# A hybrid backbone on one chip: input tiles, rope tables and scratch zeroing issued behind gates, and a planner that serves two transfer queues in turns

## The reference, cut to what matters

```python
for l in range(DEPTH):
    mod = silu_c @ w_mod[l] + b_mod[l]
    sh1, sc1, g1, sh2, sc2, g2 = split(mod, 6)
    hx = modulate(rms_norm(x, norm1_g[l]), sh1, sc1)
    if l % 2 == 0:                       # pooling || windowed attention
        out_x, out_c = even_mixer(hx, hc, mix_w_in[i], pool_w[i], ...)
    else:                                # pointwise, GLU, depthwise 31, LayerNorm, swish, pointwise
        out_x = conformer_conv(hx, *conv_args)
    x = x + g1 * out_x
    x = x + g2 * sq_relu_mlp(modulate(rms_norm(x, norm2_g[l]), sh2, sc2), mlp_w1[l], mlp_w2[l])
    # the context tokens take the same path in layers 0 and 1
return rms_norm(x, final_g)
```

## Time and profile before

| | |
|---|---|
| three runs | 3191.91, 3198.79, 3318.61 us (median 3198.79) |
| the profiled execution | 3186.52 us |
| its span, slowest core (core 4) | 3185.0 us; the others 3170.4 to 3184.0 us |
| PE busy in the span | 2963.4 us, 93% |
| DVE, ACT, POOL busy | 1890.2, 1206.6, 287.2 us |
| mean granted TensorE clock, core 4 | 0.990 |

### The profile page before, as it was taken

How to read it: one execution, slowest core, us unless ns; L and a number is a source line. 1 busy time by engine, 2 the same in 40 slices (tenths; PEclk the granted TensorE clock), 3 DMA queues, 4 the chain that set the end, 5 groups by cost and what they waited for, 6 DMA issues and landing times.

```text
span 3185.0 us, 42724 instructions; the slowest of 8 cores (3170.4 to 3185.0 us)
## 1 busy us (share of the span) xinstructions
PE 2963.4 (93%) x17933; PEld 1326.0 (42%) x18239; DVE 1890.2 (59%) x2941; ACT 1206.6 (38%) x1856; POOL 287.2 (9%) x545
## 2 busy tenths in 40 slices
PE   0699999999989999999999999999999999999997
PEld 0244344444444444444444443444443444344443
DVE  0455665665672457656567656665667346756567
ACT  1656821111264565211115658211116447411114
POOL 1102001111000000111100000011110010101000
PEclk9999999999999999999999999999999999999999
DMA  9327134444124662443422122244342472313102
GB/s 209 54 40 118 28 56 63 71 67 67 27 50 100 137 129 42 67 66 54 65 36 47 34 40 34 48 77 83 54 66 44 106 157 64 53 27 54 27 14 106
DMA packets 139968, 213.39 MB, mean 67 GB/s; under 512 B 18304, under 2 KB 66176, under 8 KB 139136
## 3 DMA queue, kind: packets, MB, share of 16 engines
q0 software_dynamic: 77904, 141.27, 28.1%
q1 hardware_dynamic: 61872, 69.38, 8.5%
HBM read 334.26 MB, written 17.56 MB: 110 GB/s over the span
## 4 chain that ended last, share of the span: by engine, by line
PE 83%; ACT 6%; DVE 6%; DMA 2%; SPq 2%; issue 1%; DVEq 0%; ACTq 0%
PE ps L157 83%; ACT ARENA L157 4%; DVE ARENA L157 4%; ACT H L157 2%; SPq L157 2%; DMA gscr<-ARENA 2%; DVE X L157 2%; DMA ARENA<-gscr 1%; DVE H L157 0%; ACT L157 0%; DVE MODV L157 0%; DVEq L1409 0%; DVE AB L157 0%; DVEq L155 0%; ACTq L155 0%
## 5 line engine op out<-in xcount | busy, mean ns | idle before, releaser
L157 PE MATMUL ps<-H,wr 128*128 128x512 bf16 (+1 forms) x7100 | 1528.0, 369 | 49.6 <-ACT ARENA L157 17.4
L157 ACT ACTIVATE ARENA<-ps 128x512 f32<-128x512 f32 (+5 forms) x939 | 586.6, 638 | 1557.9 <-PE ps L157 1537.0
L157 PEld LDWEIGHTS ps<-H,wr 128*128 128x128 bf16 x7280 | 697.1, 98 | 838.4 <-issue 34.0
L157 DVE SCALAR_TENSOR_TENSOR X<-ps,MODV,X 128x512 f32<-128x512 f32 (+1 forms) x1296 | 903.1, 718 | 203.5 <-PE ps L157 163.7
L157 PE MATMUL ps<-ARENA,wr 128*128 128x512 bf16 (+1 forms) x4511 | 1003.2, 368 | 6.7 <-DVE X L157 0.8
L157 DVE TENSOR_TENSOR ARENA<-ARENA 128x512 bf16<-128x512 f32 (+3 forms) x729 | 473.3, 661 | 577.8 <-ACT ARENA L157 577.4
L157 PEld LDWEIGHTS ps<-ARENA,wr 128*128 128x128 bf16 x4608 | 400.9, 98 | 591.5 <-DVE X L157 198.5
L157 POOL DMA_DIRECT2D wr<-w x256 | 135.7, 548 | 1326.4 <-PE ps L157 1257.5
L157 PE MATMUL ps<-ARENA 128*32 128x512 bf16 (+3 forms) x3038 | 228.8, 361 | 25.1 <-DMA ARENA<-gscr 12.8
L157 ACT ACTIVATE H<-ARENA,AB 128x512 bf16<-128x512 f32 (+1 forms) x296 | 191.2, 689 | 65.9 <-DVE ARENA L157 65.7
L157 DVE SCALAR_TENSOR_TENSOR ARENA<-X,AB,ARENA 128x512 f32<-128x512 f32 (+1 forms) x296 | 198.8, 710 | 23.4 <-ACT ARENA L157 13.8
(11 more groups left out here) (47 smaller groups left out, 715.3 us busy)
## 6 DMA issues: line engine op xcount, KB each, us to landing
wr<-w POOLq DMA_DIRECT2D x256, 256.0 KB, 6.6
wr<-w_mod POOLq DMA_DIRECT2D x192, 256.0 KB, 9.7
ARENA<-gscr SPq DMA_DIRECT2D x256, 135.0 KB, 3.6
wr<-pw POOLq DMA_DIRECT2D x48, 256.0 KB, 6.0
gscr<-ARENA SPq DMA_DIRECT2D x65, 128.0 KB, 1.9
X<-xp SPq DMA_DIRECT2D x4, 2048.0 KB, 35.2
outp<-ARENA SPq DMA_DIRECT2D x32, 256.0 KB, 2.2
ARENA<-ropet SPq DMA_DIRECT2D x8, 512.0 KB, 4.9
```

Source lines behind the costliest of these rows:

```text
L157: ins = getattr(e, it[1])(*it[2], **it[3])
```

## The change

The change has three parts.

**Gates at the start.** `load_x` and `DMA` take more keys to wait for. X0 is loaded only when the result of mod slab 1 (`modv`, 0, 1) is written; X1 only when the slab `w_u` has landed; X2 when `w_q` has landed; X3 when X1 has landed. The rope tables thereby come ahead of X0. `gpad`'s transfers also read the key (`X`, 3, 7), whose last writer by then is the mixer's output projection of tile 3; its memset is still free to go at any time.

**The planner.** Two queues (SP's, POOL's) are served in turns, piece by piece, by one server; a slab counts as four pieces, a load from the scratch as four pieces of double the bytes. A slot is counted free 0.13 us after its last user has been seen to end ("counts later bank reuse"), another 0.13 us are added before a PE operation that follows another engine, and some costs of issuing are changed.

**Pools.** The reserve of pool `f` falls from 3 to 1; the attention's `ub` pool gets a reserve of 3 and is strict (counts all older tiles); `rope_a` holds its two tiles together.

```diff
-LAT = {"pe": 0.20, "act": 0.125, "dve": 0.125, "pool": 0.15, "sp": 0.1}
+LAT = {"pe": 0.20, "act": 0.13, "dve": 0.13, "pool": 0.15, "sp": 0.1}
+LATPE = 0.13
...
+        def serve():
+            nonlocal seq
+            if dbusy[0]:
+                return
+            for k in (1 - dturn[0], dturn[0]):
+                if dqs[k]:
+                    o, last, dur = dqs[k].pop(0)
+                    dturn[0] = k
+                    dbusy[0] = True
+                    seq += 1
+                    heap_push(ev, (now + dur, seq, "free"))
+                    if last:
+                        seq += 1
+                        heap_push(ev, (now + dur + 2.0, seq, o))
+                    return
...
+                if type(o) is list:
+                    for vb in o[0].bufs:
+                        vb.left -= 1
+                        if vb.left == 0:
+                            for j in range(vb.size):
+                                vb.pool.free[vb.slot + j] = True
+                            vb.pool.settle()
+                    continue
...
-                    lat = 0.0 if (o.eng == "pe" and s_.eng == "pe") else (0.0 if o.dma is not None else LAT[o.eng])
+                    lat = LATPE if (o.eng != "pe" and s_.eng == "pe") else 0.0
...
-        f_p = gl.pool("f", NF, 512, 3)
+        f_p = gl.pool("f", NF, 512, 1)
...
-            ub_p = lay.pool("ub", 4, 256)
+            ub_p = lay.pool("ub", 4, 256, 3, True)
...
             if first:
-                load_x(1)
+                load_x(1, wu.keys())
                 norm(1, 0, 0)
+                load_x(2, wq.keys())
+                load_x(3, [("X", 1, 0)])
...
-                DMA("sp", lambda: "gr%d" % gr.slot, fl, rd + [("gpad",)], gr.keys(), 128 * 4 * w * 2, cost=1.9)
+                DMA("sp", lambda: "gr%d" % gr.slot, fl, rd + [("gpad",)], gr.keys(), 128 * 4 * w * 2 * 2, cost=1.8, pieces=4)
...
         load_x(4)
-        load_x(0)
-        for j in range(4):
-            mod_slab(0, j)
+        mod_slab(0, 0)
+        mod_slab(0, 1)
+        load_x(0, [("modv", 0, 1)])
+        mod_slab(0, 2)
+        mod_slab(0, 3)
...
-                                       for (a, b) in ((0, GL), (GL + S, GC), (GC + L, GW))], zb.keys(), [("gpad",)], 100000, cost=0.3)
+                                       for (a, b) in ((0, GL), (GL + S, GC), (GC + L, GW))], zb.keys() + [("X", 3, 7)], [("gpad",)], 3000000, cost=15.0)
```

More of the change, by code:

```diff
@@ L337, in __init__, with add @@
         self.phase_pools = []
-    def add(self, eng, emit, reads, writes, cost, dma=None, table=None, bias=0, soft=(), hold=()):
+    def add(self, eng, emit, reads, writes, cost, dma=None, table=None, bias=0, soft=(), hold=(), pieces=1):
         o = Op()
@@ L535, in schedule @@
                 done += 1
-                for vb in o.bufs:
-                    vb.left -= 1
-                    if vb.left == 0:
-                        for j in range(vb.size):
-                            vb.pool.free[vb.slot + j] = True
-                        vb.pool.settle()
+                seq += 1
+                heap_push(ev, (now + LATPE, seq, [o]))
                 for s_ in o.succ:
                     s_.npred -= 1
-                    lat = 0.0 if (o.eng == "pe" and s_.eng == "pe") else (0.0 if o.dma is not None else LAT[o.eng])
+                    lat = LATPE if (o.eng != "pe" and s_.eng == "pe") else 0.0
                     s_.ready = max(s_.ready, now + lat)
@@ L770, in PE, with DMA @@
             return R.add("pe", emit, reads, writes, cost, bias=bias, hold=hold, soft=R.after(dst))
-        def DMA(q, chan, f, reads, writes, nbytes, cost=None, soft=(), bias=0):
+        def DMA(q, chan, f, reads, writes, nbytes, cost=None, soft=(), bias=0, pieces=1):
             def emit(Sd):
@@ L775, in emit @@
                 Sd.dmas(q, Sd.chan(ch), f(), phys(reads), phys(writes))
-            return R.add(q, emit, reads, writes, cost if cost is not None else (1.0 if q == "pool" else 0.08), dma=nbytes, soft=soft, bias=bias)
+            return R.add(q, emit, reads, writes, cost if cost is not None else (0.55 if q == "pool" else 0.4), dma=nbytes, soft=soft, bias=bias, pieces=pieces)
         MMC = 0.2157
```

45 lines of the change are left out of this document (26 added, 19 removed).

## The result

The changed kernel takes 3098.38 us in the median of four runs (3097.57 to 3099.54), the kernel before 3188.41, 3191.91 and 3198.79; the ratio is 0.9704 (95% interval 0.9683 to 0.9724). In some executions of any of these kernels the cores of one die are granted a lower clock and take longer; such executions and cores are left out of every comparison here. I had forecast 3128, with 3104 to 3152 as the range: the gain is 95 us between the means, where my sum had 66, and more than half of it comes from where I had not looked.

The account below looks back on a forecast made before the run. PE was busy 2963 of 3185 us, so only 222 us of idle could be won. Terms -69 + 6 + 3 + 1 + 1 - 8 = -66 gave 3120.5; 7.5 added for runs above the profiled one made 3128, range 3104 to 3152.

Parts of the forecast that it names:

- The start: Start of layer 0: gated loads bring the first matmul with w_u from 131.3 to 62 us, a term of -69 us.
- M: The first matmul with w_u, at 131.25 us before; forecast at 62 us, bounded by 57 and 73.
- +3 ACT cover in mixer 0: Mixer of layer 0: norms of tiles 1 to 3 on ACT, now behind M, cost +3 us, bounds 0 and +17.
- +6 +3 +1: Costs put behind M: norm matmuls on PE +6.1 us, ACT's norms +3, gates behind M +1.
- The sign that I had named: Test of ACT's cover: wrong if PE's waits for ARENA tiles from ACT double between M and the MLP.
- The gates behind M, +1: Layer 0 after M: X1 there at 72 us, w_q at 74.3, both in time by 2 us; +1 us (0 to +8).
- The MLP of layer 0 idles 3.7 of 535 us, so nothing is to be had there: MLP of layer 0: PE's small idle time was taken to leave no gain there.
- The convolutions, -8: Planner's other orders, against 53.6 us of PE idle in the two convolutions: -8 us (-25 to +12).
- Zeroing, +1: Zeroing stores start when X3 is final, some 35 us of work before the slot's reuse: +1 us (0 to +10).
- The late start: Rival: slower weights' queue puts M at 70 and the mixer pays ACT's work in full; 3146 us, chance 0.18.
- The good planner: Rival: half of the convolutions' idle goes, -25 us instead of -8; 3111 us, chance 0.15.
- The slower case: Rival: fewer usable f slots double idle in the first mixer and both convolutions; 3200.5 us, chance 0.02.

Follow-up runs that it names:

- b_zt: The kernel before with only the zeroes moved to 64 columns of their own instead of a slot of f: 3152.43 us, ratio 0.9866.
- a_zt: The changed kernel, gates kept, with only the zeroes in columns of their own instead of a slot of f: 3098.40 us, ratio 0.9703.
- b_gates: The kernel before with only the gates of X0 to X3 and of the zeroing stores, old planner and pools: 3170.54 us, ratio 0.9934.
- b_zlate: The kernel before with only the zeroing (memset and three stores) moved behind the last write of X3: 3161.09 us, ratio 0.9890.
- a_f3: The changed kernel with the reserve of pool f back at 3 slots for older tiles instead of 1: 3137.77 us, ratio 0.9819.

## Why the prediction was wrong, point by point

- **The start** was right in size. M came at 64.2 against 62 (term -69, measured -65.3 as the median over cores). The landing of X0 stood 4 us too early in the sum and with it the last mod slab, but M waited last for `w_u`, whose rate carried the term. What held the start before was read rightly as well, and b_zt shows it: the slot, not the traffic. No rival said that the slot alone gives 42 of the 65 us and that the gates' other 23 are lost again behind M.
- **"+3 ACT cover in mixer 0", with bounds of 0 and +17,** is a step that failed. The mixer gave back 38 us where the sum had +6 +3 +1. I had put a price on ScalarE's work, but none on the clock nor on the tiles of VectorE behind it. The fall of the clock makes the matmuls behind a wait up to twice as long, and that price was in my own rows: 0.96 in the convolution. The sign that I had named, that the waits for ACT's ARENA tiles double, did not quite come (13.7 against 8.7), while those for DVE's H tiles did double (10.3 against 4.4); PE's busy time in the 249 us after M fell by 10.5, just past the 10 that I had allowed. In the mixer no wait is over 2.9 us; the 38 us are many small ones and the clock. In the whole program one wait after M is over 5 us, against what I had said: 8.2 us for a mod slab in the convolution of layer 1.
- **The gates behind M, +1:** X1 was there at 77.6, not 72, and PE waited neither for it nor for `w_q`.
- **"The MLP of layer 0 idles 3.7 of 535 us, so nothing is to be had there"** is the step that put the result outside the range: 51 us in the four MLPs, a place to which the sum gave nothing. PE's busy time has the load's wait in it; 49 matmuls at 11.05 us are 225.5 ns each, and 216 is what the pieces without a wait run at. 9.5 ns on each matmul stood in a row that I quoted, and I used it to price norms. That the orders of PE were the same misled me: the bank isn't in the order of the operations.
- **The convolutions, -8:** measured -7.8 and -2.7, with +1.5 in the mixer of layer 2: -9.0. That the size is right is luck. The parts that were run have opposite signs: the later free costs 25, the reserve of 1 gives about 22 back, and the transfer model with its costs of issuing gives 5 in layer 1 and takes 9 in layer 3. They make +8, not -9; the other 17 us lie in parts that no run took alone (the other latencies, the pool `ub`) or in how the parts act together. The mechanism that I named is in the trace at the head of layer 1: of the three waits of 2.17, 2.33 and 2.83 us, 1.39 and 0.25 are left. In the whole of that convolution PE's waits for ACT's tiles fell from 13.2 to 5.7 us and those for loads from the scratch from 5.7 to 2.5, and one new wait of 8.2 us for a mod slab took a part of it back.
- **Zeroing, +1:** no wait for the slot shows in the changed kernel (a_zt is equal to it). In the old planner's orders it was 5.5 us (b_gates) and 9.9 (b_zlate); the bound of +10 was the right one.
- **The rivals.** The late start named the mixer's payment for ACT's work, at 10 us on top; the whole return was 38, with the clock, and M was not late. The good planner had the right sign and the wrong place: it looked for 25 us in the convolutions. The slower case took the reserve of `f` for the danger; a_f3 shows the reverse, 39 us.
- The sum 3120.5 missed the profiled run, 3098.0, by 22.5: -51 in the MLPs, +28 in the mixer, +4 at the start, -2 in the rest, which makes -21. Two errors of opposite sign hid half of each other. The other 7.5 us of the forecast, for runs above the profiled one, did not come either: the four runs lie within 1.6 us of it.

## What to carry to other kernels

Where matmuls stand nearly without gaps, look at the weight loads' waits and at the mean time per matmul, not at the busy share: waits of a few tenths at four in ten of the small groups (188 of 480 in MLP 0) were 51 us here, 1.6% of the kernel. A resource's time of release in a planner has to include the time until its next user can see it. Work moved from before the first big matmul to behind it is not free when it runs on the engine that feeds PE there: put as much ahead as the loads cover. A planner that models the transfers more closely need not find the better order: here the coarser model was 21 us faster in the mixer. And ask of a fix what its smallest form is, here three lines for the zeroes, before gates are put around it.

## What the runs showed of the hardware

- A weight load that waits 0.32 to 0.47 us for a bank does not show as idle time of PE. It costs a little under 0.1 us: 147 such waits in MLP 1 are 12.7 us (361.3 against 348.7).
- In the mixer of layer 0 the granted clock fell to 1.2 GHz behind idle pieces of 0.5 to 2.9 us, 43 us in all; 9.9 us of added matmuls there cost no time (293 against 295 us), left PE's idle time about as it was (32 against 35 us) and brought the clock of 96 to 130 us from 0.62-0.70 to 0.75-0.95.
- MLP 1 repeats to 0.1 us from kernel to kernel: 348.7 us in all twelve kernels with the later free, 361.3 in all five without.
